# One layer of a hybrid encoder on one core: the weighting of dots and tokens in the expert schedule from block 1's attention on

## The reference, cut to what matters

```python
def _layer(h, ...):
    proj = h @ w_in                                   # 1024 tokens, d = 1024
    y_a = _gdn_branch(...)                            # gated delta rule, chunks, 4 heads
    y_b = _fox_branch(...)                            # causal attention with forget gates, 8 heads
    mix = sigmoid(gate_a) * y_a + sigmoid(gate_b) * y_b
    h = _layernorm(ALPHA * h + mix @ w_o, ln1_g, ln1_b)
    return _layernorm(ALPHA * h + _peer(h, ...), ln2_g, ln2_b)

def _peer(h, wq, keys, u_tab, v_tab):                 # tables of 16384 x 1024
    q = (h @ wq).reshape(t, 8, 2, 128)
    scores = einsum('thpd,hpnd->thpn', q, keys)
    # top 16 of 128 twice, top 16 of the 256 sums: 16 experts a head, 128 a token
    expert, gate = ...
    act = gelu(einsum('td,tkd->tk', h, u_tab[expert])) * gate
    return einsum('tk,tkd->td', act, v_tab[expert])
```

## Time and profile before

| | us |
|---|---|
| median of 3 runs | 3840.48 |
| lowest, highest | 3828.07, 3843.74 |
| the profiled execution | 3819.22 |
| span of its trace | 3817.5 |
| PE / DVE / POOL / ACT busy | 2531.7 / 2270.4 / 2222.2 / 535.7 |

### The profile page before, as it was taken

How to read it: one execution, slowest core, us unless ns; L and a number is a source line. 1 busy time by engine, 2 the same in 40 slices (tenths; PEclk the granted TensorE clock), 3 DMA queues, 4 the chain that set the end, 5 groups by cost and what they waited for, 6 DMA issues and landing times.

```text
span 3817.5 us, 36797 instructions
## 1 busy us (share of the span) xinstructions
PE 2531.7 (66%) x11992; PEld 1547.9 (41%) x11992; DVE 2270.4 (59%) x5441; ACT 535.7 (14%) x1241; POOL 2222.2 (58%) x2086
## 2 busy tenths in 40 slices
PE   8798993557976876567987876566897730133366
PEld 6685762333744544433744543333553400000011
DVE  5253898777368677554359776564455778744300
ACT  3220311112002201221002202111101000000000
POOL 1000666558445666677556666677665666666665
PEclk9898996777988988766998988777898875565577
DMA  5224998789988999999999999999999999999998
GB/s 168 79 70 150 353 404 293 270 297 362 381 312 324 375 407 363 329 352 364 416 407 338 409 407 366 338 341 369 384 405 370 395 382 374 369 368 375 374 366 314
DMA packets 367622, 1290.21 MB, mean 338 GB/s; under 512 B 39468, under 2 KB 68148, under 8 KB 362308
## 3 DMA queue, kind: packets, MB, share of 16 engines
q0 software_dynamic: 294912, 1073.87, 74.0%
q1 hardware_dynamic: 66760, 201.39, 14.3%
q10 hardware_dynamic: 5760, 12.59, 0.9%
HBM read 1274.72 MB, written 12.98 MB: 337 GB/s over the span
## 4 chain that ended last, share of the span: by engine, by line
PE 27%; DVE 22%; POOL 16%; issue 14%; DMA 8%; another core or an unknown queue 7%; DVEq 4%; ACT 2%; ACTq 0%; SPq 0%; POOLq 0%
PE banks L1453 12%; DVE ring L1118 11%; POOL ring L752 7%; POOL ring L740 6%; PE banks L1442 6%; DMA ring<-in_ev,idxT 5%; PE banks L1463 4%; POOL arena L752 2%; PE banks L1721 2%; DVE arena L1118 2%; DMA ring<-in_eu,eidx 1%; PE banks L1503 1%; POOL arena L740 1%; DMA wslot<-in_w_mix 1%
## 5 line engine op out<-in xcount | busy, mean ns | idle before, releaser
L740 POOL DMA_INDIRECT ring<-in_eu,eidx x925 | 1043.8, 1128 | 899.5 <-DVE eidx L1411 406.4
L752 POOL DMA_INDIRECT ring<-in_ev,idxT x880 | 937.8, 1066 | 543.5 <-issue 249.3
L1442 PE MATMUL banks<-ring,wide 128*32 128x512 f32 x3520 | 673.2, 799 | 443.1 <-DMA ring<-in_ev,idxT 294.0
L1118 DVE CUSTOM_DVE_ANT_0 ring<-ring,h_cur 128x1024 f32<-128x1024 f32 x768 | 906.6, 1221 | 88.3 <-DMA ring<-in_eu,eidx 60.0
L1453 PE MATMUL banks<-arena,wslot 128*128 128x256 f32 (+1 forms) x3248 | 757.9, 390 | 43.3 <-issue 22.3
L1453 PEld LDWEIGHTS banks<-arena,wslot 128*128 128x128 f32 (+1 forms) x3248 | 624.5, 195 | 203.5 <-issue 96.0
L1442 PEld LDWEIGHTS banks<-ring,wide 128*32 128x32 f32 x3520 | 139.0, 133 | 783.7 <-issue 764.6
L1463 PE MATMUL banks<-arena 128*128 128x128 f32 x1408 | 231.6, 328 | 65.4 <-ACT arena L907 42.0
L1118 DVE CUSTOM_DVE_ANT_0 ring<-ring,banks 128x1024 f32<-128x1024 f32 x157 | 187.2, 1219 | 116.1 <-DMA ring<-in_eu,eidx 91.3
L1463 PEld LDWEIGHTS banks<-arena 128*128 128x128 f32 x1408 | 212.1, 235 | 98.2 <-ACT arena L907 51.2
L1442 PE MATMUL banks<-arena,wide 128*32 128x512 f32 x576 | 181.1, 812 | 98.9 <-DMA ring<-in_ev,idxT 64.5
(11 more groups left out here) (289 smaller groups left out, 2843.1 us busy)
## 6 DMA issues: line engine op xcount, KB each, us to landing
wslot<-in_w_pq SPq DMA_DIRECT2D x64, 576.0 KB
wslot<-in_w_mix SPq DMA_DIRECT2D x24, 1536.0 KB
wslot<-in_w_qkv SPq DMA_DIRECT2D x48, 512.0 KB
wslot<-in_w_fqk SPq DMA_DIRECT2D x32, 512.0 KB
wslot<-in_w_out SPq DMA_DIRECT2D x8, 2048.0 KB
ring<-in_eu,eidx POOLq DMA_INDIRECT x925
ring<-in_ev,idxT POOLq DMA_INDIRECT x880
wslot<-in_w_z SPq DMA_DIRECT2D x16, 512.0 KB
```

Source lines behind the costliest of these rows:

```text
L740: pool.indirect_dma_start(out=place(UPOS[k]), out_offset=None, in_=eu, in_offset=bass.IndirectOffsetOnAxis(ap=eidx[:, n % (2 * TT), c // T ...
L752: pool.indirect_dma_start(out=place(VPOS[k]), out_offset=None, in_=ev, in_offset=bass.IndirectOffsetOnAxis(ap=idxT[:, n % (2 * TT), t:t + ...
L1118: dve.tensor_tensor_reduce(out=row, in0=row, in1=h_cur[:, n % 3, :] if n < NT - TT else hp[n % 2], scale=1.0, scalar=0.0, op0=ALU.mult, op ...
L1442: last = pe.matmul(BY[k][32 * j:32 * j + 32, :], wide32[:, at:at + 32], place(VPOS[4 * q + j])[:, k * 512:(k + 1) * 512], start=(m == 0), ...
```

## The change

Behind unit `second` the planner no longer lets the dots grow in proportion to the shares, but the sum of dots and tokens. `steep` is what one dot brings in sum while the dots go from 160 to 256 (1 and 56/96 tokens), above 256 it is 2; `gone` is the sum that is due, and `want` the dots that belong to it. The three limits, the rule for the tokens, the counts at unit 234 and from unit 548 on stay.

```diff
             if n < second:
                 want = P + round((SECOND - P) * run / levels)
             else:
-                want = SECOND + round((T * (NB - 1) - SECOND) * (run - levels) / (total - levels))
+                steep = 1 + (P - LAG - VSECOND) / (T - SECOND)
+                whole = (T - SECOND) * steep + 2 * T * (NB - 2)
+                gone = whole * (run - levels) / (total - levels)
+                want = SECOND + round(gone / steep)
+                if want > T:
+                    want = T + round((gone - (T - SECOND) * steep) / 2)
```

## The result

The change makes the kernel slower, and by three times what was forecast: 3928.19 us (median of 4, 3914.82 to 3958.67) against 3836.36 (median of 4, 3828.07 to 3843.74). The ratio is 1.024, 95% interval 1.0208 to 1.0271, +92 us; the forecast was 3872, the range ended at 3905. So their traces are 139 us apart, 47 more than the times; what follows reads where that difference arises, and takes its size from the times.

A forecast was written before the change was run, and what follows sets the result against it. Transfers were taken to bound the kernel where rows are late, DVE at the beginnings of choices. The terms 17 - 13 + 35 - 3 - 10 + 5 = +31 us on 3840.5 gave 3872, range 3830 to 3905.

The forecast's parts named there:

- engines set the pace: Rival: an added gather in block 1's choices costs nothing, only dots taken from DVE count; -23 us, 3817; chance 0.11.
- there is room in the transfers: Rival: low GB/s at full DMA share is room, 21 us in each of two block 1 stretches; -7, 3833; chance 0.2.
- term 1: Block 1's attention and merge, units 234 to 280: 28 more gathers, 37 us less 20 of ring head start, +17 us.
- term 2: Start of block 1's choices, units 281 to 293: 13 dots fewer on DVE, less some 2 us gate wait; -13 us.
- Term 3: Block 1's seven choices, units 294 to 342: 26 more gathers at 1.33 us where rows are late; +35 us.
- term 4: Block 2's delta rule, attention and merge, units 342 to 414: 5 gathers fewer, half their price gained; -3 us.
- Term 5: Start of block 2's choices, units 414 to 427: 9 dots fewer on DVE, 20 gathers given back unneeded; -10 us.
- Term 6: From unit 428 on: 13 more gathers up to unit 474, +17, then 13 fewer up to 548, -12; +5 us.
- bursts: Rival: in block 1's choices 24 places fall due behind two units, ring of 15, DVE waits; +26 us, 3898; chance 0.12.
- the criterion set ahead: Block 1's last choice: within 15 us of its old end, gathers have room; 60 or more later, it is bursts.
- the rule weighed: Skill rule: read HBM utilization, not DMA occupancy; with 425 GB/s, some 30 us to spare in each of two block 1 stretches.

The follow-up runs named there:

- e5: Kernel before up to block 2's second choice, the change's tables from unit 428 on; 3695.14 us, ratio 1.0012 to before.
- e3: The change for units 234 to 293 alone, tables of before from unit 294 on; 3703.22 us, ratio 1.0025 to before.
- e9: Before spread, with 8 dots and the tokens that follow fewer due by the last choices of blocks 1 and 2; ratio 1.0003 to before.
- e10: Before spread, with up to 12 dots fewer in block 1's merge, given back by its first choice; ratio 0.9978 to before.
- e11: Before spread, with fewer dots and tokens both by the last choices of blocks 1 and 2 and in block 1's merge; ratio 0.9986 to before.

## Why the prediction was right or wrong

- **Direction and reading of the bound: right.** Transfers are the pace in block 1's choices and behind them, and a gather added in the choices costs its transfer. The opposite, *engines set the pace*, is out, and so is *there is room in the transfers*: 26 gathers more, spread, cost 31.6 and 34.8 us over before spread (two jobs).
- **Terms 1 and 2** (17 - 13 = +4): +7 in the run of the front alone. In the traces of the result the second choice ends 21 us later than before in place of 4, in that of the change on the second kind 6 more than in e5 from block 0's last choice on. The share ahead of the first choice is 0.38, as forecast well under 0.76, and POOL issues nothing at all there. The two terms can be told apart at the end of the merge, where the same instruction of DVE stands at these two times, before and in the change:

```profile
1057.24 0.69 DVE L1330 SCALAR_TENSOR_TENSOR arena<-arena,banks 128x512 f32<-128x512 f32 x1 [4.24 <-PE banks L1721]
1091.54 0.69 DVE L1335 SCALAR_TENSOR_TENSOR arena<-arena,banks 128x512 f32<-128x512 f32 x1 [2.74 <-PE banks L1726]
```

  It is 34 us later, 3 of them from ahead of block 1. So term 1 measured +31 where it had +17, and what follows gave back 14, as term 2 has it (13). On the second kind, in four pairs of traces, the end of the merge is 18 to 28 us later and the second choice 5 to 12. The cover that term 1 took off, 20 us, was too much in all but one of them. The 2 us for the gate did not come: DVE does it at 1121.68 without a wait, and in the earlier trace rows the table load stands behind the GELU and not ahead of it.
- **Term 3** (+35, up to unit 342): 24 between the landmarks with spread dots, 40 (312 against 271) as the change has it. Its price of a gather, 1.33, fits (1.1 to 1.3 measured). Between the ends of the second and the last choice lie six choices and not seven, and the landmark stands ahead of the last choice's own dots, so part of the term lies behind it: seven dots stand behind that unit in the change, spread or not, and two or three before. Between spread kernels DVE's instructions are 24 us later at the landmark and some 37 us later 15 us on. That is also the cause of **term 4's** miss (-3): the time from the last choice of block 1 to the first of block 2 grew by 12 and 17.
- **Term 5** (-10): from first to second choice of block 2 32 us in place of 42 on the second kind, -9, and -7 in the result. Between the two choices it is right (the dots fewer are 8 and not 9), but from the layer norm of block 2 to the second choice, which is the term, it is 82 in place of 87, not 77. The 20 gathers given back there gained nothing of their own, as said.
- **Term 6** (+5): +4. Its parts in the traces, e5 against e3, are +20 in the choices of block 2 (275 against 255) and -8 from there to block 3; these two add up to more than the times give. On the chip of the result they were +36 and +9: there nothing came back.
- **The step that failed** is the rival *bursts*, left out of the sum and given 0.12 because "the ring is refilled while DVE chooses". It is refilled then, with up to 15 gathers; what I had not seen is that during the burst POOL, in order, stands behind a slot of tokens that PE holds (9.33 us in the timeline above), so the dots' slots are not refilled. Bursts cost 25 and 27 us in the change (59 against 34 and 32), and before had some of it itself (spreading gains 11 and 7), so 14 to 20 of the change's price are new bursts, where the rival said +26. With it the sum would have been 31 + 26 = +57, and +59 was measured on the second kind. That this fits is in part luck: the rival had DVE wait 96 us for rows in the choices, and it waits 73 (44 in e5). The other part is quantity: 31 forecast, 34 + 11 = 45 and 32 + 7 = 39 between spread kernels. What the forecast lacks there is mostly in terms 3 to 5: 22 forecast, 32 and 35 between spread kernels.
- By the criterion set ahead (last choice of block 1 "60 or more later, it is the bursts") the trace of the result, 69 later, named them at once. But on the second kind the change has its last choice 43 us later than e5 (1480 and 1437), with bursts just the same: the mark was reached with the help of the chip.
- **What no term has** is the chip: 92 us on that of the result, 59 on another kind, so 33 of the 92 us have no shown cause. The range was made as if the rows of one trace held for every execution's idle time.

Of the rule weighed: the Trainium skill, Perfetto Trace Analysis, section Identifying the Most-Contended Engine, has it that the occupancy of sixteen DMA engines misleads. As to the rate the traces agree: in block 3, before on the first kind of chip has 373 GB/s at a share of 0.96,

```profile
3100.00:3800.00 700.00, 234.23 (x980) 49.28 (x981) 315.83 (x526) 5.19 (x9) 463.82 (x494) 0.60 0.96 373
```

and before spread on the second 416 at 1.03:

```profile
3100.00:3650.00 550.00, 194.23 (x982) 39.40 (x986) 236.30 (x386) 2.79 (x6) 399.51 (x425) 0.63 1.03 416
```

As to room they don't: e9 has 16 gathers more than e10 behind block 1's last choice, at 367 and 368 GB/s, and takes 27 us more for them (e11 19), so 370 GB/s at a full share was not room that more gathers could use. What the share does tell, where it falls: 0.94 to 0.97 in a stretch where both users wait for rows was the sign of the holes.

## What to carry to other kernels

Where one ring serves two consumers and its producer is in order, a burst of one consumer frees places that the producer can't reach until the other has caught up; the transfers then run dry with the same total of work. Spread the uses of both evenly before moving any quantity; that was worth 7 to 11 us here, and moving 16 gathers between two stretches of full transfers nothing. And look for windows in which waits for rows and a DMA share well under one stand together: there suspect the order of the gathers before the bandwidth.

## What the hardware showed that I had not expected

The same kernel takes 3812 and 3836 us in two jobs and 3686 to 3696 in four others, 3 to 4% apart. Block 0 takes nearly the same on both kinds (its last choice ends at 836 to 841 on the first kind and at 824 to 829 on the second). Over half of the difference is in block 3 from its first choice on, where all kernels of this study have the same tables: 901 us in before, 832 in e5, whose spans are 118 apart. A price measured on one chip need not hold on another: 1.024 and 1.0265 against 1.0168.

TensorE's granted clock goes with the bursts: 0.81 in the choices of before bunched and 0.88 in those of before spread. Its waits there are longer with bursts (21.1 us against 9.2), and the next work begins at the lower level: in the change, behind an idle 5.60 us, the 16 matmuls at 1241.4 take 3.64 us, where those at 1228.5 took 1.92; the clock from 1240 to 1250 is 0.52. Over the whole stretch PE is busy for no longer with bursts (199.5 and 200.2 us), and DVE's longer waits for rows alone (25 us) come to about the 26 us. So nothing here needs the clock as a cause, but it was not tried apart.
